# Loading x whole on two queues and halving the first weight slab in a two-block transformer kernel on one core

## What is computed

```python
xn = rmsnorm(h, norm_mix_g[l])
u = jnp.einsum('bsd,de->bse', xn, w_in[l])      # 1024 x 7168 weights
q, k, v, xr, gr, ga, gb = jnp.split(u, splits, axis=-1)
...                                             # attention, RG-LRU, merge, FFN
h = x + (g_a * ya + g_b * yb) @ w_o[l]
```

## Time and profile before

| | |
|---|---|
| median of three runs | 962.61 us (962.27 to 963.04) |
| the profiled execution's own time | 962.92 us |
| its span, from the first to the last instruction | 961.1 us |
| what lies around the span | 1.8 us |
| TensorE clock granted, mean over the span | 0.998 |
| HBM to SBUF and back, whole span | 169.32 MB, mean 176 GB/s |

### The profile page before, as it was taken

One profiled execution on the slowest core, in us unless ns is written; L12 is line 12 of the kernel. 1 busy time (PEld: TensorE's weight loads), 2 busy tenths in 40 slices (PEclk: granted clock), 3 DMA queues, 4 the chain that ended last, 5 costly groups with the idle time before them and its releaser, 6 DMA issues.

```text
span 961.1 us, 14426 instructions
## 1 busy us (share of the span) xinstructions
PE 945.8 (98%) x4870; PEld 802.5 (84%) x4870; DVE 506.7 (53%) x849; ACT 489.0 (51%) x771; POOL 287.8 (30%) x150
## 2 busy tenths in 40 slices
PE   8999999999999999999999999999998999999997
PEld 7999988888888888888888888888888878888886
DVE  5858964656754443422744443357488773443332
ACT  6577455554464444433744444447346665444442
POOL 1000000000034443443244444654412044344432
PEclk9999999999999999999999999999999999999999
DMA  7755565445556656878566566645503346566552
GB/s 238 240 180 165 173 193 177 143 129 175 178 171 193 184 175 188 282 219 224 166 196 191 178 188 185 228 150 174 165 22 125 101 150 194 176 190 188 189 189 74
DMA packets 132770, 169.32 MB, mean 176 GB/s; under 512 B 16707, under 2 KB 88430, under 8 KB 132598
## 3 DMA queue, kind: packets, MB, share of 16 engines
q1 hardware_dynamic: 132566, 168.67, 57.0%
q10 hardware_dynamic: 160, 0.07, 0.0%
HBM read 167.61 MB, written 1.10 MB: 176 GB/s over the span
## 4 chain that ended last, share of the span: by engine, by line
PE 94%; DVE 2%; ACT 2%; issue 1%; POOL 0%; DVEq 0%; POOLq 0%; ACTq 0%
PE acc L842 25%; PE acc L844 25%; PE acc L843 25%; PE tp L918 4%; PE acc L900 3%; PE acc L902 3%; PE acc L904 3%; PE sc L994 1%; PE acc L1186 1%; DVE w_lo L1261 1%; ACT w_hi L501 1%; ACT junk L513 0%; PE sc L1145 0%; PE tp L1014 0%; PE sc L936 0%
## 5 line engine op out<-in xcount | busy, mean ns | idle before, releaser
L501 ACT ACTIVATE w_hi<-w_raw 128x1024 fp32r<-128x1024 f32 x301 | 317.7, 1059 | 357.4 <-PE acc L844 318.5
L1261 DVE TENSOR_TENSOR w_lo<-w_raw,w_hi 128x1024 fp32r<-128x1024 f32 x197 | 249.5, 1271 | 293.9 <-ACT w_hi L501 292.8
L1891 POOL TENSOR_TENSOR w_lo<-w_raw,w_hi 128x1024 fp32r<-128x1024 f32 x104 | 251.1, 2415 | 395.4 <-ACT w_hi L501 395.4
L842 PE MATMUL acc<-w_hi,xt_hi 128*128 128x512 f32 (+1 forms) x736 | 292.4, 397 | 0.6 <-DVE w_lo L1261 0.3
L844 PE MATMUL acc<-w_lo,xt_hi 128*128 128x512 f32 (+1 forms) x736 | 287.0, 390 | 0.0
L843 PE MATMUL acc<-w_hi,xt_lo 128*128 128x512 f32 (+1 forms) x736 | 286.3, 389 | 0.0
L844 PEld LDWEIGHTS acc<-w_lo,xt_hi 128*128 128x128 f32 x736 | 138.1, 188 | 29.3
L842 PEld LDWEIGHTS acc<-w_hi,xt_hi 128*128 128x128 f32 x736 | 138.3, 188 | 28.5 <-DVE w_lo L1261 0.9
L843 PEld LDWEIGHTS acc<-w_hi,xt_lo 128*128 128x128 f32 x736 | 138.4, 188 | 27.2
L842 PE MATMUL acc<-w_hi,hid_hi 128*128 128x512 f32 x264 | 103.3, 391 | 0.0
L844 PE MATMUL acc<-w_lo,hid_hi 128*128 128x512 f32 x264 | 102.8, 389 | 0.0
(11 more groups left out here) (212 smaller groups left out, 917.7 us busy)
## 6 DMA issues: line engine op xcount, KB each, us to landing
w_raw<-in_ffn_w_gu SPq DMA_DIRECT2D x172, 256.0 KB
w_raw<-in_w_in SPq DMA_DIRECT2D x68, 512.0 KB
w_raw<-in_w_ffn_in SPq DMA_DIRECT2D x88, 256.0 KB
w_raw<-in_ffn_w_down SPq DMA_DIRECT2D x44, 512.0 KB
w_raw<-in_w_ffn_out SPq DMA_DIRECT2D x22, 512.0 KB
w_raw<-in_w_rnn_out SPq DMA_DIRECT2D x8, 512.0 KB
w_raw<-in_w_attn_out SPq DMA_DIRECT2D x8, 512.0 KB
w_raw<-in_w_o SPq DMA_DIRECT2D x8, 512.0 KB
```

What stands on the lines that cost most here:

```text
L501: act.activation(w_hi[:, b, :], w_raw[:, b, :], ACT.Copy).then_inc(hi_done[b], 1)
L842: pe.matmul(o, hi[:, k, rows], wh, start=first and n == 0, stop=False)
L1261: dve.tensor_tensor(w_lo[:, b, :], w_raw[:, b, :], w_hi[:, b, :].bitcast(F32), ALU.subtract).then_inc(lo_done[b], 1)
L1891: pool.tensor_tensor(w_lo[:, b, :], w_raw[:, b, :], w_hi[:, b, :].bitcast(F32), ALU.subtract).then_inc(lo_done[b], 1)
```

## The change

SP issues the first row tile of x (tokens 0 to 127, all 1024 columns, 512 KB), then the first half of slab 0 (256 KB, row tile j = 0), its second half (256 KB, j = 1), then slabs 1, 2 and 3. ACT issues the second row tile of x (512 KB) ahead of the identity and the gain's rows. Both tiles of x count on one semaphore, and each `turn_x` waits for both. ACT rounds slab 0 in two halves and DVE makes its residual in two halves, each with a semaphore. PE waits for the first half's residual, runs the 12 products with j = 0 over all four output tiles, waits for the second, and runs the 12 with j = 1. All other slabs and groups have their products in the order of before.

```diff
-            for q in range(4):
-                if q < 3:
-                    cols = (slice(0, 256), slice(256, 512), slice(512, D))[q]
-                    sp.dma_start(h[:, :, cols], xv[:, :, cols]).then_inc(x_landed[q], 16)
+            sp.dma_start(h[:, 0, :], xv[:, 0, :]).then_inc(x_landed, 16)
+            sp.dma_start(w_raw[:, 0, 0:W], w_in[0:P, 3 * D:3 * D + W]).then_inc(half_landed, 16)
+            sp.dma_start(w_raw[:, 0, W:2 * W], w_in[P:2 * P, 3 * D:3 * D + W]).then_inc(raw_landed[0], 32)
+            for q in range(1, 4):
                 slab(q, rect(q, w_in, 256 * q, 3 * D))
...
+            act.dma_start(h[:, 1, :], a["x"].rearrange("b (m p) d -> p (b m) d", p=P)[:, 1, :]).then_inc(x_landed, 16)
             act.dma_start(ident[:], a["c_ident"]).then_inc(ident_landed, 16)
...
                 split(X["x"] + n, (2 * n, 2 * n + 1), gain_x, xt_hi)
-                feed(n, 1)
+                if n == 0:
+                    act.wait_ge(half_landed, 16)
+                    act.activation(w_hi[:, 0, 0:W], w_raw[:, 0, 0:W], ACT.Copy).then_inc(half_hi, 1)
+                    act.wait_ge(raw_landed[0], 32)
+                    act.activation(w_hi[:, 0, W:2 * W], w_raw[:, 0, W:2 * W], ACT.Copy).then_inc(hi_done[0], 1)
+                else:
+                    feed(n, 1)
...
                 for q in range(4):
                     r = (s + q) % RING
-                    pe.wait_ge(lo_done[r], (s + q) // RING + 1)
+                    if s + q == 0:
+                        pe.wait_ge(half_lo, 1)
+                    else:
+                        pe.wait_ge(lo_done[r], (s + q) // RING + 1)
...
+                    if s + q == 0:
+                        for c in range(4):
+                            products(r, q, c, 0)
+                        pe.wait_ge(lo_done[r], 1)
+                        for c in range(4):
+                            mm = products(r, q, c, 1)
...
             def turn_x(n):
-                pe.wait_ge(x_landed[min(n, 2)], 16)
+                pe.wait_ge(x_landed, 32)
                 turn_tiles(X["x"] + n, h, (2 * n, 2 * n + 1))
...
                 split(X["x"] + n, (2 * n, 2 * n + 1), gain_x, xt_hi, xt_lo, HI["x"] + 2 * n)
-                feed(n, 1)
+                if n == 0:
+                    dve.wait_ge(half_hi, 1)
+                    dve.tensor_tensor(w_lo[:, 0, 0:W], w_raw[:, 0, 0:W], w_hi[:, 0, 0:W].bitcast(F32),
+                                      ALU.subtract).then_inc(half_lo, 1)
+                    dve.wait_ge(hi_done[0], 1)
+                    dve.tensor_tensor(w_lo[:, 0, W:2 * W], w_raw[:, 0, W:2 * W], w_hi[:, 0, W:2 * W].bitcast(F32),
+                                      ALU.subtract).then_inc(lo_done[0], 1)
+                else:
+                    feed(n, 1)
```

More of the change, by code:

```diff
@@ L246, in build @@
     ssq_done, ms_done, rs_done = sem("ssq_done"), sem("ms_done"), sem("rs_done")
-    x_landed = [sem(f"x_landed{c}") for c in range(3)]
+    x_landed = sem("x_landed")
+    half_landed, half_hi, half_lo = sem("half_landed"), sem("half_hi"), sem("half_lo")
     ident_landed, par_landed = sem("ident_landed"), sem("par_landed")
@@ L887, in group_turned, with products @@
                 banks = acc[g % 2 * 2:g % 2 * 2 + 2]
+                def products(r, q, c, j):
+                    k, cols = 2 * q + j, slice(j * W + c * P, j * W + (c + 1) * P)
+                    o = banks[c // 2][:, c % 2 * T:(c % 2 + 1) * T]
+                    pe.matmul(o, w_hi[:, r, cols], xt_hi[:, k, :], start=q == 0 and c % 2 == 0 and j == 0,
+                              stop=False, skip_group_check=True)
+                    pe.matmul(o, w_hi[:, r, cols], xt_lo[:, k, :], start=False, stop=False,
+                              skip_group_check=True)
+                    return pe.matmul(o, w_lo[:, r, cols], xt_hi[:, k, :], start=False, stop=q == 3 and j == 1,
+                                     skip_group_check=True)
                 for q in range(4):
                     r = (s + q) % RING
-                    pe.wait_ge(lo_done[r], (s + q) // RING + 1)
+                    if s + q == 0:
+                        pe.wait_ge(half_lo, 1)
+                    else:
+                        pe.wait_ge(lo_done[r], (s + q) // RING + 1)
                     if ready is not None:
@@ L894, in group_turned @@
                         wait_bank(pe, g, 1)
-                    for b in range(2):
-                        for c in (2 * b, 2 * b + 1):
-                            for j in range(2):
[L898 to L909, removed]
+                    if s + q == 0:
[5 more added lines that the diff above has]
+                    else:
+                        for c in range(4):
+                            for j in range(2):
+                                mm = products(r, q, c, j)
+                            if c == 1 and q == 3:
+                                mm.then_inc(acc0_full[g % 2], 1)
+                    mm.then_inc(slab_used[r], 1)
                     if q in after:
```

## The result

The changed kernel took 964.55 us at the median of 20 runs (963.83 to 966.30), the kernel before 962.98 us in the 20 runs beside it (962.27 to 964.29). The ratio is 1.002 with a 95% interval of 1.0014 to 1.0026. It is slower by 1.6 us: less than the 1.9 us that the prediction set as the limit of what can be told, but with 20 runs on each side the interval is clear of 1. The profiled execution took 963.98 us with a span of 962.2, 1.1 us over the 961.1 of before.

What follows compares the result with a forecast made beforehand. PE, busy 98% of the span, bounds the kernel, so its first product decides: x 1.6 us later, the path 0.97 us shorter, product 0.62 us later. Against medians 962.61 + 0.6 = 963.2 us, range 962.1 to 964.9.

Steps and rivals of the forecast that it cites:

- no change that can be measured: Forecast for the whole kernel: 0.6 us slower, below the 0.2% (1.9 us) that a measurement can tell; same 0.84.
- if SP's queue gets as much meanwhile: Assumption before the transposes: while ACT's queue passes 0.59 MB, SP's passes as much, 1.19 MB in all.
- B: Rival, x slow: transposes start at 7.45 at the lower clock, first product 1.8 us later, 964.4 us; chance 0.13.
- D: Rival: ACT's queue served below an even share, x's second tile, identity and gain land late, 964.3 us; chance 0.05.
- When x is there: Step before the first product: x's transposes start at 6.7 against 5.11, 1.6 us later.
- The fit of 2.0 us plus bytes at 436 GB/s: Set-aside estimate for the loads before the start: 1.19 MB landed at 5.5, first product at 8.8, gain 0.4 us.
- From the transposes to the product: Step from x's transposes to slab 0's first product: 3.15 us against 4.12, or 3.54 at the lower clock.
- The covers: Claimed free: ACT's rounding under 0.5 us of cover, second residual under 1.44 us of products, slab 1 with 0.6 us.
- Rival C: Rival: PE's standstills leave slab 0's 24 products at 1.2 GHz, costing 2.3 us more, 965.5 us; chance 0.12.
- the holes of before were of the same order: Argument against a clock loss at the first products: PE's earlier holes, 0.7 and 1.1 us, were similar and the clock held.
- A: Rival, x fast: transposes start at 6.05, first product at 9.2 as before, 962.6 us; chance 0.15.

Runs made afterwards that it cites:

- the first part alone: Kernel before with only x loaded whole on two queues, second tile ahead of the identity, slab 0 in one piece: 966.41 us against 963.00, ratio 1.0033.

## Why the prediction was wrong

The time, 964.55 us, lies inside the range, and a later start was forecast. But the forecast "no change that can be measured" was wrong: 1.57 us were lost where 0.6 were forecast. Of the 0.95 us between them 0.33 are the start of the transposes, 0.10 the path from there to the product, and the rest, about 0.5, is the clock. Two steps failed: the clock was left out of the sum, and "if SP's queue gets as much meanwhile" does not hold for the identity. That the time is in the range is luck in part: its upper end came from B and D, and neither happened. (B and A with 0.3 us of spread give 964.7 and 962.3, not 964.9 and 962.1.)

**When x is there.** I put the start of the transposes at 6.7, from an even share of bytes between the queues. It was 7.03. The composition was further off than the sum. x itself landed at 5.85, for the engines moved 422 and 418 GB/s from 3 to 5 us. Then the identity behind it took 0.93 us more, for which I had given the price of its bytes. The failed step is "if SP's queue gets as much meanwhile": in bytes that holds only for rows of like size. What the two queues had moved by 6.4 us, when all but the last 4 of the 304 packets of ACT's queue had passed:

```profile
q1 hardware_dynamic: 374, 0.96, 48.1%
q10 hardware_dynamic: 300, 0.59, 24.6%
```

SP's queue moved 0.96 MB beside the 0.59, so 1.55 MB had to pass and not 1.19. That 6.7 was so near is luck: the engines were faster (1.55 MB by 6.4 us, where 1.13 MB had passed by 6.0 in the rows that I used), and from the last rows to the identity's landing at 6.78 it took under 0.4 us, where I had 1.05. With the identity elsewhere (two experiments) the transposes started at 5.86 and 5.88. On the number of queues the Trainium skill ("DMA: Bandwidth & Descriptors", Rules for kernel authors) was right: two queues brought x no sooner than one.

```profile
3.00:4.00 1.00, 1.00 (x4) 0.76 (x3) 0.00 (x0) 0.80 (x2) 0.43 (x1) 1.00 1.03 422
4.00:5.00 1.00, 0.98 (x3) 0.26 (x1) 0.00 (x0) 0.00 (x0) 0.00 (x0) 1.00 1.02 418
```

These are stretches of the changed kernel. The fit of 2.0 us plus bytes at 436 GB/s, which I set aside, is one that the Trainium skill ("DMA: Bandwidth & Descriptors", Anatomy of one DMA) gives for single transfers issued by GpSimd. As an estimate for these it gave 5.5 for the landing: close for x (5.54 and 5.85), and 1.3 us too early for the identity behind it.

**From the transposes to the product.** Predicted 3.15, measured 3.25: 0.75 to `xt_hi` (7.03 to 7.78) where I took 0.63, 0.97 to `xt_lo` where I took 0.96, and 1.53 for `xt_lo`, the half residual and PE (8.75 to 10.28) where I took 1.56. The halving gives 0.61 us; I had costed it at 0.58 (0.65 in place of 1.23). The covers held: ACT's second half, the second residual and slab 1 made nobody wait. The clock had risen before the transposes, as I took it. The first two steps together give 10.28 in place of 9.85: +1.05 us where +0.62 was forecast.

**Rival C, the clock.** This is the larger miss. I priced it as all or nothing, at 2.3 us with a chance of 0.12, and left it out of the forecast. It is a matter of the single execution. The profiled one shows nothing of it: its products are 0.12 us apart. But nine of 20 executions had a span of 963.3 or more, and filling the holes with zeros took the spread away (962.0 to 962.5) and 0.45 us off the median. So a case with a small chance should have been a term of the sum: about half the executions, 1.1 to 2.3 us each. The argument against it, "the holes of before were of the same order", was also too weak. The longest holes of before were 0.6 and 1.1 us and those of the change 1.9 and 1.3, and the kernel before has late executions too, 17 of 93. The remark that 0.2% is what a measurement can tell hid the rest: with 20 runs a side the interval reached 0.6 us to either side.

**Rivals A, B and D.** A (level with before) came true only when the identity was moved. B's time, 964.4, is the nearest of all by luck: its start of the transposes, 7.45, is further off than 6.7, and in the profiled execution they ran at the higher clock. D had the right thing, ACT's queue late, but in the wrong form: x was served evenly, and only the small load behind it was not.

## What to carry to other kernels

Before moving a large load ahead of a small one, ask who waits for the small one: 64 KB behind 512 KB landed 0.93 us after the last of x here, and 64 KB ahead of 512 KB, on a queue beside a full one, let these land at 7.8 us in place of 5.5. At the head of the full queue the 64 KB were in time, and the start came 1.15 us sooner. A shorter chain behind a load pays only if every step that stands in line ahead of it in the engine's program is fed by then. Where a change lets TensorE stand still for a microsecond more, look at the spans of many executions and not at one profile, and try a few matmuls over zeros to price the clock.

## What the runs showed of the hardware

A queue with rows of 512 bytes beside a full queue with rows of 4 KB got half of the packets (81 of 163 in 1 us) and 11% of the bytes (0.04 of 0.36 MB). Beside each other, two queues with rows of 4 KB got 0.33 and 0.30 MB in 1.5 us.

The granted clock fell once more after it had risen: in the first part alone it was 1.00 until 8.2 us and 0.50 until 15, after a standstill of 2.1 us from 4.95 on. In the profiled execution of the changed kernel, which stood still for 1.9 us from 4.98 on, it stayed at 1.00, and its transposes and products show the higher level. Each is one execution.

The column of the granted clock says 1.00 at the start of these traces, also where TensorE runs at the lower level. A stretch of the kernel with the identity first:

```profile
9.00:11.00 2.00, 2.00 (x8) 1.51 (x7) 0.98 (x3) 1.94 (x5) 0.00 (x0) 1.00 0.99 366
```

Its timeline, in the same stretch:

```profile
9.60 1.06 PE L938 MATMUL tp<-ident,h 128*128 128x128 f32 x4
...
10.46 1.06 PE L956 MATMUL sc<-sb 128*128 128x256 f32 x2
```

At the higher clock they take 0.60 us each. That lower clock lasted here into the products, 0.21 us apart (11.93, 12.14, 12.36). So at the start of these traces only durations tell its level.
